# Recurrent heads: the scores of neighbouring pairs as VectorE products summed by ones, and the sums of output squares in a rounded part and its rest

## The chip, the cores and the metric

One core of a Trainium2 chip. The metric is the device time of one execution in microseconds; it was measured in three runs of the kernel before. A profile of one further execution shows where the time goes.

## The reference

A two-layer decoder trunk for 1024 new prompt tokens and 8 sampled tokens. Layer A is a gated linear recurrence (HGRN2) with 8 heads of 128 keys and 128 values, layer B is differential attention; each has a SwiGLU FFN behind it. What matters here is the mixer of layer A, cut to its core:

```
q, f, i, g = jnp.split(xn @ w_in, 4, axis=-1)
fg = lb + (1.0 - lb) * jax.nn.sigmoid(f)
qh, kh, logf, vh = jax.nn.silu(q), 1.0 - fg, jnp.log(fg), i
...
scores = jnp.einsum('bthk,bshk,btshk->bhts', qc, kc, decay)   # decay = exp(b_t - b_s), s <= t
...
o = rmsnorm(o, gnorm.reshape(HG_HEADS, HG_DV))
o = o * jax.nn.silu(g)
return o @ w_out, s_new
```

All of it is float32. A score of token t and an earlier token s is the sum over the 128 keys of q_t, k_s and the product of the forget gates from s + 1 to t.

## The kernel before, in words

Activations lie with features on partitions and the T = 1032 tokens (1024 of the prompt and 8 samples) along the free axis. A projection works on slabs of weights of 128 x 2048 numbers. SyncE loads a slab, GpSimd (POOL) splits it into a rounded part `w_hi` and the rest `w_lo`, and TensorE (PE) makes three rounded (float32r) products per tile with activations split in the same way (`split_product`, lines 728 to 730). A group is one output chunk of 128 features over one of NT = 3 tiles of TS = 344 tokens: 8 x 3 = 24 such products. The other products of the stage are full float32.

The recurrent heads come first in the program. Every head needs 12 projection groups (0 to 2 q, 3 to 5 the gate, 6 to 8 f, 9 to 11 v). PE's order is written out by hand in `hg_head(h)`: the 12 groups of head h + 1 (`next_part`) stand between the small steps of head h, so that PE has work while the other engines prepare the next small step. Every step waits on semaphores that count up. The steps of a head:

- `hg_norm(h - 1)`, line 887: three full-precision products of a matrix of ones with the squares of the last head's output, `RS`. Each gives the sum over 128 features, for 344 tokens. ACT takes Ln and Exp of it (`hg_rstd`, lines 1560 and 1562), DVE multiplies the output by it (`hg_norm`, line 1980), POOL gates it (line 688).
- `hg_diagonal`, line 907: 8 products of K and Q of 128 tokens each; only the diagonals are kept. DVE then multiplies Q by the forget gate F (line 2054) and copies the diagonals into the scores `SA` by a mask (line 2055).
- `hg_turn_v`, line 896: 8 transposes of V into banks 5 and 6, which the sums of `hg_norm` also use, so it waits for the Ln (`hg_oln`). ACT copies them to `VT` (line 1587).
- `hg_level(h, l)` for l = 0 to 6, line 921: the scores between the two halves of blocks of 2, 4, ... 128 tokens, 8 products each. Level 0 is that of neighbouring tokens: it computes 128 x 64 scores per block of 128 tokens, and one per odd token is kept. After each level DVE multiplies decays into Q and K (`hg_spread`, lines 2006 and 2007), makes the next block decays (`hg_totals`, line 1995) and copies the wanted scores (`hg_take`, line 2015).
- `hg_spread_v`, `hg_turn_k`, `hg_sample`, `hg_outer` and `hg_output`: the sample's state, the states of the blocks of 128 and the output, in banks 3 and 4. ACT copies the output to `O` (line 1615) and squares it into `RS` (line 1621).

The last head is `hg_last`: there are no next groups, and the groups of the output projection (`woa_early`, which needs the first six heads' gated outputs reloaded, cast by ACT in line 1571 and split by DVE in line 1942) stand between its steps. Its first, `woa_first`, follows level 0 and takes the six chunks one by one. The table `WOA_AT` says how many groups follow each level. DVE adds their results to the residual (`woa_add`, line 1949). At the end PE has `hg_norm(7)`, six more early groups and `out_late`. `hg_head` of ACT (line 1573 on) and of DVE (line 2049 on) are the same heads as their engines' queues have them; an engine does them in this order and each waits for its own semaphores.

## Time and profile before

| | us |
|---|---|
| median of 3 runs | 2818.02 (2816.6 to 2820.09) |
| the profiled execution | 2818.19 |
| its span, first to last instruction | 2816.5 |
| PE busy | 2750.8 (98%) |
| DVE busy | 1192.1 (42%) |
| ACT busy | 574.3 (20%) |
| POOL busy | 1102.3 (39%) |
| mean granted clock of PE, as a share | 0.990 |

The profile's busy time of an engine is the time in which at least one of its instructions ran. PE's products overlap: one starts while the one before still drains, so what a product costs is the distance from its start to the next one's, not its own duration. A full-precision product is recorded as two instructions (x6 for three products). PEld is PE's weight load and PEq its instruction queue. The bracket behind a row of a timeline gives how long the engine sat idle before it, and what released it.

### The profile page before, as it was taken

Reading aid. Unit: us, or ns where it says so; the run is one execution under the profiler, and the core shown is the slowest. Engines: PE = TensorE matmul, PEld = TensorE weight load, DVE = VectorE, ACT = ScalarE, POOL = GpSimd, SP = SyncE. Lnnn points to the kernel's source line nnn. Section 1 sums busy time; section 2 is a strip of 40 time slices with the busy share of each in tenths; the row PEclk is TensorE's granted clock in tenths of the full one; section 3 lists DMA queues with packets and bytes.
Section 4 is the critical chain, followed back from the end, with each engine's and each line's share of the span. In section 5 each row is a group of like instructions: output and inputs, shape, how many; then the busy total and the mean of one; then the engine's idle time right before and its main releaser. Section 6 shows DMA issues by size and latency. Waiting matters only on the chain.

```text
span 2816.5 us, 43463 instructions
## 1 busy us (share of the span) xinstructions
PE 2750.8 (98%) x17561; PEld 2668.1 (95%) x17561; DVE 1192.1 (42%) x2257; ACT 574.3 (20%) x1182; POOL 1102.3 (39%) x962
## 2 busy tenths in 40 slices
PE   7999999989999999999999999988999999999999
PEld 6999999989999999999999888876899999999999
DVE  4355554455333333333361334476433333333335
ACT  4222222223200000000030233464130000000003
POOL 4333333333444443333346324313533334444334
PEclk8999999999999999999999999999999999999999
DMA  3211111121111111111122111165211111111111
GB/s 106 61 54 54 54 54 54 47 92 54 46 46 45 46 45 47 56 48 45 46 92 68 43 57 52 40 216 189 93 50 45 46 45 46 45 46 45 52 54 61
DMA packets 202241, 175.06 MB, mean 62 GB/s; under 512 B 6290, under 2 KB 185093, under 8 KB 202062
## 3 DMA queue, kind: packets, MB, share of 16 engines
q1 hardware_dynamic: 162592, 141.67, 16.1%
q10 hardware_dynamic: 39470, 30.78, 3.4%
q8 instruction: 140, 2.29, 0.3%
q14 instruction: 39, 0.32, 0.0%
HBM read 147.06 MB, written 25.36 MB: 61 GB/s over the span
## 4 chain that ended last, share of the span: by engine, by line
PE 92%; DVE 4%; ACT 1%; POOL 1%; issue 1%; DMA 0%; ACTq 0%; SPq 0%; PEld 0%; DVEq 0%; PEldq 0%; POOLq 0%
PE ps L728 27%; PE ps L730 26%; PE ps L729 26%; PE ps L921 3%; PE ps L1181 2%; PE ps L1161 2%; DVE act_lo L1942 1%; PE ps L1269 1%; PE ps L907 1%; PE ps L954 1%; PE ps L963 1%; PE ps L887 0%; DVE k_page L2285 0%; PE ps L947 0%; PE ps L1139 0%
## 5 line engine op out<-in xcount | busy, mean ns | idle before, releaser
L728 PE MATMUL ps<-act_hi,w_hi 128*128 128x344 f32 (+2 forms) x3808 | 1243.9, 327 | 26.8 <-DVE act_lo L1914 7.5
L729 PE MATMUL ps<-act_lo,w_hi 128*128 128x344 f32 (+2 forms) x3808 | 1220.7, 321 | 0.0
L730 PE MATMUL ps<-act_hi,w_lo 128*128 128x344 f32 (+2 forms) x3808 | 1220.6, 321 | 0.0
L677 POOL TENSOR_TENSOR w_hi<-w_stage,ones 128x512 fp32r<-128x512 f32 (+1 forms) x412 | 428.4, 1070 | 1285.8 <-PEq L778 1120.4
L728 PEld LDWEIGHTS ps<-act_hi,w_hi 128*128 128x128 f32 x3808 | 718.9, 189 | 44.1 <-issue 32.3
L729 PEld LDWEIGHTS ps<-act_lo,w_hi 128*128 128x128 f32 x3808 | 718.9, 189 | 3.5 <-issue 1.7
L730 PEld LDWEIGHTS ps<-act_hi,w_lo 128*128 128x128 f32 x3808 | 718.8, 189 | 0.0
L681 POOL TENSOR_TENSOR w_lo<-w_stage,w_hi 128x512 fp32r<-128x512 f32 (+1 forms) x412 | 541.5, 1345 | 8.1
L728 PE MATMUL ps<-h_hi,w_hi 128*128 128x344 f32 x1056 | 339.3, 321 | 1.1 <-DVE resid L2123 1.1
L729 PE MATMUL ps<-h_lo,w_hi 128*128 128x344 f32 x1056 | 337.3, 319 | 0.0
L730 PE MATMUL ps<-h_hi,w_lo 128*128 128x344 f32 x1056 | 337.2, 319 | 0.0
L2123 DVE TENSOR_TENSOR resid<-resid,ps 128x344 f32<-128x344 f32 x504 | 258.1, 513 | 180.6 <-PE ps L730 180.2
L2100 DVE TENSOR_TENSOR ps<-ps,rstd 128x344 f32<-128x344 f32 x132 | 68.9, 524 | 391.2 <-PE ps L730 380.5
L1651 ACT ACTIVATE silu_gate<-ps 128x344 f32<-128x344 f32 x132 | 60.1, 458 | 807.2 <-DVE ps L2100 807.2
L2103 DVE TENSOR_TENSOR ps<-ps,rstd 128x344 f32<-128x344 f32 x132 | 69.2, 524 | 363.3 <-PE ps L730 363.3
L728 PEld LDWEIGHTS ps<-h_hi,w_hi 128*128 128x128 f32 x1056 | 198.4, 188 | 2.9 <-DVE resid L2123 2.3
L730 PEld LDWEIGHTS ps<-h_hi,w_lo 128*128 128x128 f32 x1056 | 198.7, 188 | 0.0
L729 PEld LDWEIGHTS ps<-h_lo,w_hi 128*128 128x128 f32 x1056 | 198.5, 188 | 0.0
L1656 ACT CAST h_hi<-ps 128x344 fp32r<-128x344 f32 x132 | 58.9, 446 | 445.3 <-DVE ps L2106 445.3
L921 PEld LDWEIGHTS ps<-hg_q,hg_k 128*128 128x128 f32 (+4 forms) x896 | 93.8, 177 | 4.5 <-issue 3.7
L921 PE MATMUL ps<-hg_q,hg_k 128*128 128x64 f32 (+4 forms) x896 | 94.7, 258 | 2.0 <-DVE hg_scores L2055 1.7
L694 POOL TENSOR_TENSOR state_sample<-state_sample,hg_f 128x1024 f32<-128x1024 f32 x8 | 16.6, 2071 | 193.8 <-DMA state_sample<-in_state_hgrn 193.8
(298 smaller groups left out, 2179.3 us busy)
## 6 DMA issues: line engine op xcount, KB each, us to landing
w_stage<-in_w_gate_up SPq DMA_DIRECT2D x88, 512.0 KB, 5.0
w_stage<-in_w_down SPq DMA_DIRECT2D x44, 512.0 KB, 4.2
w_stage<-in_w_in_a SPq DMA_DIRECT2D x32, 512.0 KB, 5.2
w_stage<-in_w_kv SPq DMA_DIRECT2D x16, 512.0 KB, 4.3
v_page<-in_cache_v SPq DMA_DIRECT2D x16, 512.0 KB, 6.2
w_stage<-in_w_out_b SPq DMA_DIRECT2D x12, 512.0 KB, 4.4
k_page<-in_cache_k SPq DMA_DIRECT2D x10, 512.0 KB, 5.3
x_spill<-resid ACTq DMA_DIRECT2D x8, 516.0 KB, 2.9
```

What stands on the lines that cost most here:

```text
L677: last = g.tensor_tensor(hi[:, part], WST[:, part], ones[:, 0:1].to_broadcast([P, quarter]), ALU.mult)
L681: last = g.tensor_tensor(lo[:, part], WST[:, part], hi[:, part], ALU.subtract)
L728: pe.matmul(out, wh, xh, start=first, stop=False)
L729: pe.matmul(out, wh, xl, start=False, stop=False)
L730: return pe.matmul(out, wl, xh, start=False, stop=last)
L921: last = pe.matmul(PS[0:KEYS[l], 3 + l % 2, c * 64:(c + 1) * 64], K[h % 2][:, c * P:c * P + KEYS[l]], q[:, c, :, 1, :], start=True, stop=True)
L1161: last = pe.matmul(PS[:, bank + k0 // 512, 0:k1 - k0], QA[:, 2 * h + c, n * P:(n + 1) * P], KTB[h % 2][:, c, k0:k1], start=True, stop=True)
L1651: a.activation(SIL[:, tile(t)], PS[:, t, 0:TS], ACT.Silu).then_inc(ffn_silu, 1)
L1656: a.copy(HH[par][:, k, tile(t)], PS[:, 3 + t, 0:TS]).then_inc(ffn_hh, 1)
L2100: v.tensor_tensor(PS[:, t, 0:TS], PS[:, t, 0:TS], RS[:, tile(t)], ALU.mult).then_inc(ffn_gscaled, 1)
L2103: v.tensor_tensor(PS[:, 3 + t, 0:TS], PS[:, 3 + t, 0:TS], RS[:, tile(t)], ALU.mult).then_inc(ffn_uscaled, 1)
L2123: v.tensor_tensor(X[:, m, tile(t)], X[:, m, tile(t)], PS[:, 6 + q % 2, 0:TS], ALU.add).then_inc(ffn_down_free, 1)
```

## The change

It does three things, for each head.

1. Level 0 is no longer made from K and Q by PE. DVE multiplies the forget gate of the odd tokens, K of the even and Q of the odd ones into `PR` (two products of 128 x 512), ahead of the diagonal. PE sums them over the keys with one full-precision product with the ones (128 x 512), which gives each score in every row; the same mask picks it. `hg_spread(h, 0)` no longer waits for PE's level 0, and `hg_take` gets that wait.
2. The squares of the output are rounded by ACT into `OHI` (in the memory of `HKT`, k_tok), and DVE takes the rest, in place, into `RSL`. PE sums both with rounded ones: 6 rounded products for 3 full ones.
3. The order: on PE group 0 of the next head comes before `hg_norm(h - 1)`, and group 1 before `hg_turn_v`; ACT takes group 0 before `hg_rstd` and group 1 before the copies of V. In `hg_last` nothing of this order changes.

```
--- before.py
+++ after.py
@@ -109,6 +109,7 @@
         WL = [place(f"w_lo{s}", [P, SLAB], F32R) for s in range(2)]
         rs_at = cursor[0]
         RS = place("rstd", [P, T])
+        RSL = at("square_lo", [P, T], F32R, rs_at)
         ident = place("ident", [P, P])
         ones = place("ones", [P, P])
         pick = place("pick", [P, 16])
@@ -178,6 +179,7 @@
         hg_k_ready = sem("hg_k_ready")
         hg_diag_full = sem("hg_diag_full")
         hg_qp_ready = sem("hg_qp_ready")
+        hg_pairs_ready = sem("hg_pairs_ready")
         hg_tot = sem("hg_tot")
         hg_p_full = sem("hg_p_full")
         hg_spread_done = sem("hg_spread_done")
@@ -199,6 +201,7 @@
         hg_os_full = sem("hg_os_full")
         hg_os_copied = sem("hg_os_copied")
         hg_osq = sem("hg_osq")
+        hg_osq_lo = sem("hg_osq_lo")
         hg_on_full = sem("hg_on_full")
         hg_oln = sem("hg_oln")
         hg_ors = sem("hg_ors")
@@ -337,12 +340,16 @@
         assert w[0] >= arena + (NB + 1) * D * 4
         VT = part("v_tok", [P, NB, P])
         SA = part("hg_scores", [P, SEQ])
-        HKT = part("k_tok", [P, NB, P])
+        hkt_at = w[0]
+        OHI = part("o_square_hi", [P, T], F32R)
+        HKT = at("k_tok", [P, NB, P], F32, hkt_at)
         ST = part("hg_states", [P, NB, P])
         S0 = part("state_sample", [P, DEC, P])
         TOT = [None] + [part(f"block_decay{l}", [P, SEQ >> l]) for l in range(1, NL + 1)]
         lmask = [part(f"level_mask{l}", [P, P // 2], BF16) for l in range(NL)]
         dmask = part("diagonal_mask", [P, P], BF16)
+        PR = part("pair_products", [P, SEQ // 2])
+        onesr = part("ones_rounded", [P, P], F32R)
 
         SQN = 6
         SQ = at("squares", [P, SQN, T], F32, arena + 65536 - SQN * T * 4)
@@ -649,6 +656,7 @@
             step(g.affine_select(out=dmask[:], in_=dmask[:], compare_op=ALU.not_equal, fill=1.0,
                                  base=0, pattern=[[-1, P]], channel_multiplier=1))
             step(g.memset(SA[:], 0.0))
+            step(g.tensor_tensor(onesr[:], ones[:], ones[:], ALU.mult))
             g.memset(stat[:], 0.0).then_inc(consts, 1)
 
             def split(n, cols=SLAB, gain=None):
@@ -881,10 +889,13 @@
 
             def hg_norm(h):
 
-                pe.wait_ge(hg_osq, h + 1)
+                pe.wait_ge(hg_osq, 2 * h + 2)
                 pe.wait_ge(hg_state_ready, (h + 1) * NB)
                 for t in range(NT):
-                    last = pe.matmul(PS[:, 5 + t, 0:TS], ones[:], RS[:, tile(t)], start=True, stop=True)
+                    pe.matmul(PS[:, 5 + t, 0:TS], onesr[:], OHI[:, tile(t)], start=True, stop=False)
+                pe.wait_ge(hg_osq_lo, h + 1)
+                for t in range(NT):
+                    last = pe.matmul(PS[:, 5 + t, 0:TS], onesr[:], RSL[:, tile(t)], start=False, stop=True)
                 last.then_inc(hg_on_full, 1)
 
             def hg_turn_v(h):
@@ -911,11 +922,13 @@
             def hg_level(h, l):
 
                 half = LEVELS[l] // 2
-                if l:
-                    pe.wait_ge(hg_spread_done, h * NL + l)
-                else:
-                    pe.wait_ge(hg_qp_ready, h + 1)
-                pe.wait_ge(hg_s_ready, h * (NL + 1) + max(l, 1))
+                if l == 0:
+                    pe.wait_ge(hg_pairs_ready, 2 * h + 2)
+                    pe.wait_ge(hg_s_ready, h * (NL + 1) + 1)
+                    pe.matmul(PS[:, 3, :], ones[:], PR[:], start=True, stop=True).then_inc(hg_p_full, 1)
+                    return
+                pe.wait_ge(hg_spread_done, h * NL + l)
+                pe.wait_ge(hg_s_ready, h * (NL + 1) + l)
                 q = Q[h % 2][:, 0:SEQ].rearrange("p (c n u m) -> p c n u m", c=NB, u=2, m=half)
                 for c in range(NB):
                     last = pe.matmul(PS[0:KEYS[l], 3 + l % 2, c * 64:(c + 1) * 64], K[h % 2][:, c * P:c * P + KEYS[l]],
@@ -1056,12 +1069,12 @@
 
                 def next_part(q):
                     hg_part(h + 1, q)
+                next_part(0)
                 if h:
                     hg_norm(h - 1)
-                next_part(0)
                 hg_diagonal(h)
+                next_part(1)
                 hg_turn_v(h)
-                next_part(1)
                 for l in range(NL):
                     hg_level(h, l)
                     if l == 1:
@@ -1572,8 +1585,6 @@
 
             def hg_head(h, more):
 
-                if more and h:
-                    hg_rstd(h - 1)
                 act.wait_ge(hg_os_full, h)
                 act.wait_ge(s1_out, h * 16)
                 act.dma_start(S0[:], state_in[h]).then_inc(s0_in, 16)
@@ -1581,12 +1592,15 @@
                     hg_rstd(h - 1)
                 if more:
                     hg_evacuate(h + 1, 0)
+                    if h:
+                        hg_rstd(h - 1)
+                    hg_evacuate(h + 1, 1)
                 act.wait_ge(hg_o_full, h * 2)
                 for u in range(2):
                     act.wait_ge(hg_vt_full, h * 2 + u + 1)
                     a.copy(VT[:, 4 * u:4 * u + 4, :], PS[:, 5 + u, :].rearrange("p (b n) -> p b n", b=4)).then_inc(hg_vt_ready, 1)
                 if more:
-                    for q in range(1, 9):
+                    for q in range(2, 9):
                         hg_evacuate(h + 1, q)
                     hg_gates(h + 1)
                 if not more:
@@ -1598,6 +1612,7 @@
                 act.wait_ge(hg_s1_ready, (h + 1) * DEC)
                 act.dma_start(state_out[h], S0[:]).then_inc(s1_out, 16)
                 act.wait_ge(hg_kv_full, h)
+                act.wait_ge(hg_on_full, h)
                 for u in range(2):
                     act.wait_ge(hg_kst_full, h * 2 + u + 1)
                     a.copy(HKT[:, 4 * u:4 * u + 4, :], PS[:, 5 + u, :].rearrange("p (b n) -> p b n", b=4)).then_inc(hg_kst_ready, 1)
@@ -1619,6 +1634,9 @@
                 act.wait_ge(hg_os_copied, h + 1)
                 act.wait_ge(hg_on, h)
                 a.activation(RS[:], O[:], ACT.Square).then_inc(hg_osq, 1)
+                act.wait_ge(hg_osq, 2 * h + 1)
+                act.wait_ge(hg_kv_full, h + 1)
+                a.copy(OHI[:], RS[:]).then_inc(hg_osq, 1)
                 if more:
                     hg_evacuate(h + 1, 11)
 
@@ -1974,6 +1992,11 @@
                     sum_square(norm_ph, m)
 
 
+            def hg_square_rest(h):
+
+                dve.wait_ge(hg_osq, 2 * h + 2)
+                v.tensor_tensor(RSL[:], RS[:], OHI[:], ALU.subtract).then_inc(hg_osq_lo, 1)
+
             def hg_norm(h):
 
                 dve.wait_ge(hg_ors, h + 1)
@@ -2000,7 +2023,10 @@
                 fine = TOT[l] if l else F
                 tot = fine[:, 0:2 * n].rearrange("p (n u) -> p n u", u=2)
                 q, k = hg_pairs(Q[h % 2][:, 0:SEQ], l)[:, :, 1, :], hg_pairs(K[h % 2][:, 0:SEQ], l)[:, :, 0, :]
-                dve.wait_ge(hg_p_full, h * NL + l + 1)
+                if l:
+                    dve.wait_ge(hg_p_full, h * NL + l + 1)
+                else:
+                    dve.wait_ge(hg_pairs_ready, 2 * h + 2)
                 dve.wait_ge(hg_qp_ready, h + 1)
                 dve.wait_ge(hg_spread_done, h * NL + l)
                 v.tensor_tensor(q, q, tot[:, :, 0:1].to_broadcast([P, n, half]), ALU.mult)
@@ -2011,6 +2037,7 @@
                 keys = KEYS[l]
                 s = hg_pairs(SA[0:keys, :], l)[:, :, 1, :].rearrange("p (c n) m -> p c n m", c=NB)
                 m = lmask[l][0:keys, :].bitcast(U16).rearrange("p (n m) -> p n m", m=LEVELS[l] // 2).unsqueeze(1)
+                dve.wait_ge(hg_p_full, h * NL + l + 1)
                 dve.wait_ge(hg_s_ready, h * (NL + 1) + l + 1)
                 v.copy_predicated(s, m.to_broadcast([keys, NB, P // LEVELS[l], LEVELS[l] // 2]),
                                   PS[0:keys, 3 + l % 2, :].rearrange("p (c n m) -> p c n m", c=NB, m=LEVELS[l] // 2)
@@ -2050,6 +2077,13 @@
 
                 dve.wait_ge(hg_k_ready, h + 1)
                 hg_totals(h, 0)
+                if h:
+                    hg_square_rest(h - 1)
+                odd, even = (hg_pairs(x[:, 0:SEQ], 0)[:, :, u, 0] for x, u in ((F, 1), (K[h % 2], 0)))
+                v.tensor_tensor(PR[:], odd, even, ALU.mult).then_inc(hg_pairs_ready, 1)
+                dve.wait_ge(hg_pairs_ready, 2 * h + 1)
+                v.tensor_tensor(PR[:], PR[:], hg_pairs(Q[h % 2][:, 0:SEQ], 0)[:, :, 1, 0], ALU.mult).then_inc(hg_pairs_ready, 1)
+                dve.wait_ge(hg_pairs_ready, 2 * h + 2)
                 dve.wait_ge(hg_diag_full, h + 1)
                 v.tensor_tensor(Q[h % 2][:, 0:SEQ], Q[h % 2][:, 0:SEQ], F[:, 0:SEQ], ALU.mult).then_inc(hg_qp_ready, 1)
                 v.copy_predicated(SA[:].rearrange("p (c n) -> p c n", c=NB),
@@ -2080,6 +2114,7 @@
             hg_head(HEADS - 1, last=True)
             woa_add(12, 6)
             woa_rest(EARLY, XL32[:, EARLY, :])
+            hg_square_rest(HEADS - 1)
             hg_norm(HEADS - 1)
             dve.wait_ge(hg_on, HEADS)
             v.tensor_tensor(O[:], O[:], G[(HEADS - 1) % 2][:], ALU.mult).then_inc(hg_head_done, 1)
```

What stands in DVE's queue where head 1 begins (behind the states of head 0 and before the diagonal scores are used), before; `hg_f` is the forget gate, `block_decay` the products of neighbouring gates:

```order
L1995 TENSOR_TENSOR block_decay_96<-hg_f 128x512 [waits hg_tot,hg_k_ready]
L2054 TENSOR_TENSOR hg_q_83<-hg_q_83,hg_f 128x1024 [waits hg_diag_full]
L2055 COPY_PREDICATED hg_scores<-diagonal_mask,ps 128x1024
L2006 TENSOR_TENSOR hg_q_83<-hg_q_83,hg_f 128x512 [waits hg_spread_done,hg_qp_ready,hg_p_full]
L2007 TENSOR_TENSOR hg_k_85<-hg_k_85,hg_f 128x512
L1995 TENSOR_TENSOR block_decay_97<-block_decay_96 128x256 [waits hg_tot]
L2015 COPY_PREDICATED hg_scores<-level_mask_103,ps 128x512 [waits hg_s_ready]
```

And after the change:

```order
L2018 TENSOR_TENSOR block_decay_98<-hg_f 128x512 [waits hg_tot,hg_k_ready]
L1998 TENSOR_TENSOR square_lo<-rstd,o_square_hi 128x1032 [waits hg_osq]
L2083 TENSOR_TENSOR pair_products<-hg_f,hg_k_86 128x512
L2085 TENSOR_TENSOR pair_products<-pair_products,hg_q_84 128x512 [waits hg_pairs_ready]
L2088 TENSOR_TENSOR hg_q_84<-hg_q_84,hg_f 128x1024 [waits hg_diag_full,hg_pairs_ready]
L2089 COPY_PREDICATED hg_scores<-diagonal_mask,ps 128x1024
L2032 TENSOR_TENSOR hg_q_84<-hg_q_84,hg_f 128x512 [waits hg_spread_done,hg_qp_ready,hg_pairs_ready]
L2033 TENSOR_TENSOR hg_k_86<-hg_k_86,hg_f 128x512
L2018 TENSOR_TENSOR block_decay_99<-block_decay_98 128x256 [waits hg_tot]
L2042 COPY_PREDICATED hg_scores<-level_mask_105,ps 128x512 [waits hg_s_ready,hg_p_full]
```

Three instructions came in ahead of the wait for the diagonal (`hg_diag_full`), and the wait for PE's level 0 (`hg_p_full`) moved from the spread to the copy of the scores.

DVE's queue at the end of the last head, behind its states, before (`resid` are the adds of the output projection, `act_lo` the rests of its operands):

```order
L1949 TENSOR_TENSOR resid<-resid,ps 128x344 [waits woa_full] x6
L1942 TENSOR_TENSOR act_lo<-act_whole,act_hi 128x1032 [waits hi_ready]
L1980 SCALAR_TENSOR_TENSOR hg_o<-hg_o,vectors,rstd 128x1032 [waits hg_ors]
L2085 TENSOR_TENSOR hg_o<-hg_o,hg_gate_87 128x1032 [waits hg_on]
L1949 TENSOR_TENSOR resid<-resid,ps 128x344 [waits woa_full] x4
```

And after the change:

```order
L1967 TENSOR_TENSOR resid<-resid,ps 128x344 [waits woa_full] x6
L1960 TENSOR_TENSOR act_lo<-act_whole,act_hi 128x1032 [waits hi_ready]
L1998 TENSOR_TENSOR square_lo<-rstd,o_square_hi 128x1032 [waits hg_osq]
L2003 SCALAR_TENSOR_TENSOR hg_o<-hg_o,vectors,rstd 128x1032 [waits hg_ors]
L2120 TENSOR_TENSOR hg_o<-hg_o,hg_gate_88 128x1032 [waits hg_on]
L1967 TENSOR_TENSOR resid<-resid,ps 128x344 [waits woa_full] x4
```

The rest of the squares stands behind the sixth add, whose group is the last that PE makes before the norm, and behind the rest of chunk 6. On PE the norm of the last head, between the 18th and 19th group of the output projection, reads after the change:

```order
L738 MATMUL ps<-act_hi,w_lo_57 128x344
L895 MATMUL ps<-o_square_hi,ones_rounded 128x344 [waits hg_state_ready,hg_osq]
L895 MATMUL ps<-o_square_hi,ones_rounded 128x344 x2
L898 MATMUL ps<-square_lo,ones_rounded 128x344 [waits hg_osq_lo]
L898 MATMUL ps<-square_lo,ones_rounded 128x344 x2
L736 MATMUL ps<-act_hi,w_hi_56 128x344 [waits woa_free,operand_split,w_split]
```

Where three full-precision products stood that waited for the squares alone, there are now three and three, and the second three wait for DVE.

## Rows read from the trace of the kernel before

**Rows 1.** The page, chain of work that ended last, by engine.
```profile
PE 92%; DVE 4%; ACT 1%; POOL 1%; issue 1%; DMA 0%; ACTq 0%; SPq 0%; PEld 0%; DVEq 0%; PEldq 0%; POOLq 0%
```

**Rows 2.** Busy time by stretch, one head: from:to, us, busy us, PE's clock, DMA.
```profile
292.00:361.60 69.60, 69.60 (x509) 68.71 (x509) 35.30 (x47) 19.55 (x28) 25.18 (x18) 1.00 0.20 55
```

**Rows 3.** PE's waits from 60 to 700 us: total, times, longest.
```profile
PE ps L728 <- DVE act_lo L1942: 5.5, 2, 5.2
PE ps L728 <- DVE resid L1949: 2.7, 2, 1.9
PE ps L921 <- DVE hg_scores L2055: 1.7, 1, 1.7
```

**Rows 4.** Timeline of PE at a norm: start, us, instruction.
```profile
291.82 1.90 PE L887 MATMUL ps<-rstd,ones 128*128 128x344 f32 x6
...
293.71 0.32 PE L729 MATMUL ps<-act_lo,w_hi 128*128 128x344 f32 x1
...
294.34 0.32 PE L730 MATMUL ps<-act_hi,w_lo 128*128 128x344 f32 x1
```

**Rows 5.** Timeline of PE at level 0 of the same head.
```profile
303.76 1.89 PE L921 MATMUL ps<-hg_q,hg_k 128*128 128x64 f32 x16
...
305.71 0.32 PE L729 MATMUL ps<-act_lo,w_hi 128*128 128x344 f32 x1
```

**Rows 6.** Timeline of PE, two 512-column sums with the ones in the FFN.
```profile
719.36 1.02 PE L744 MATMUL ps<-rstd,ones 128*128 128x512 f32 x2
...
721.24 0.32 PE L729 MATMUL ps<-act_lo,w_hi 128*128 128x344 f32 x1
```

**Rows 7.** Timeline of ACT in one head: table load, Ln, square.
```profile
292.50 1.28 ACT L1560 ACT_TABLE_LOAD   x1
293.79 1.12 ACT L1560 ACTIVATE rstd<-ps,eps_col 128x1032 f32<-128x1032 f32 x1
...
358.49 1.06 ACT L1621 ACTIVATE rstd<-hg_o 128x1032 f32<-128x1032 f32 x1
```

**Rows 8.** Timeline of DVE in one head, from the diagonal on.
```profile
299.31 2.90 DVE L2054 TENSOR_TENSOR hg_q<-hg_q,hg_f 128x1024 f32<-128x1024 f32 x1 [14.14 <-PE ps L907]
302.12 1.32 DVE L2055 COPY_PREDICATED hg_scores<-diagonal_mask,ps 128x1024 f32<-128x1024 uint16 x1
...
354.11 0.68 DVE L1995 TENSOR_TENSOR block_decay<-hg_f 128x512 f32<-128x512 f32 x1
```

**Rows 9.** Timeline of POOL, the first split of weights.
```profile
19.76 1.04 POOL L677 TENSOR_TENSOR w_hi<-w_stage,ones 128x512 fp32r<-128x512 f32 x1 [8.23 <-DMA w_stage<-in_w_in_a]
```

**Rows 10.** The chain of waits, front of the last head: start, us, what.
```profile
576.47 1.98 PE ps L921 x16
...
578.47 0.69 DVE hg_q L2006
...
582.37 1.04 DVE act_lo L1942
...
583.43 11.60 DVE act_lo L1942 x5
```

**Rows 11.** Timeline of ACT, the Exp in the front of the last head.
```profile
574.60 1.06 ACT L1562 ACTIVATE rstd<-rstd 128x1032 f32<-128x1032 f32 x1
```

**Rows 12.** Timeline of PE, DVE and POOL at the last norm.
```profile
660.05 1.90 PE L887 MATMUL ps<-rstd,ones 128*128 128x344 f32 x6
...
660.68 1.23 DVE L1942 TENSOR_TENSOR act_lo<-act_whole,act_hi 128x1032 fp32r<-128x1032 f32 x1
...
662.00 4.04 POOL L677 TENSOR_TENSOR w_hi<-w_stage,ones 128x512 fp32r<-128x512 f32 x4 [14.94 <-PEq L778]
```

**Rows 13.** Timeline of PE, behind a wait early in the stage.
```profile
49.24 0.40 PE L728 MATMUL ps<-act_hi,w_hi 128*128 128x344 f32 x1 [2.19 <-ACT hg_q L1543]
```

**Rows 14.** Busy time by stretch, columns as in rows 2.
```profile
50.00:54.00 4.00, 4.00 (x18) 4.00 (x17) 0.00 (x0) 0.00 (x0) 4.00 (x4) 0.57 0.00 0
600.00:602.00 2.00, 0.79 (x5) 0.82 (x6) 2.00 (x5) 0.00 (x0) 0.10 (x1) 1.00 0.28 49
```

More of the change, by code:

```diff
@@ L882, in hg_norm @@
             def hg_norm(h):
-                pe.wait_ge(hg_osq, h + 1)
+                pe.wait_ge(hg_osq, 2 * h + 2)
                 pe.wait_ge(hg_state_ready, (h + 1) * NB)
                 for t in range(NT):
-                    last = pe.matmul(PS[:, 5 + t, 0:TS], ones[:], RS[:, tile(t)], start=True, stop=True)
+                    pe.matmul(PS[:, 5 + t, 0:TS], onesr[:], OHI[:, tile(t)], start=True, stop=False)
+                pe.wait_ge(hg_osq_lo, h + 1)
+                for t in range(NT):
+                    last = pe.matmul(PS[:, 5 + t, 0:TS], onesr[:], RSL[:, tile(t)], start=False, stop=True)
                 last.then_inc(hg_on_full, 1)
@@ L1573, in hg_head @@
             def hg_head(h, more):
-                if more and h:
-                    hg_rstd(h - 1)
                 act.wait_ge(hg_os_full, h)
@@ L1588, in hg_head @@
                 if more:
-                    for q in range(1, 9):
+                    for q in range(2, 9):
                         hg_evacuate(h + 1, q)
@@ L1621, in hg_head @@
                 a.activation(RS[:], O[:], ACT.Square).then_inc(hg_osq, 1)
+                act.wait_ge(hg_osq, 2 * h + 1)
+                act.wait_ge(hg_kv_full, h + 1)
+                a.copy(OHI[:], RS[:]).then_inc(hg_osq, 1)
                 if more:
```

47 lines of the change are left out of this document (38 added, 9 removed).

## The prediction

> **What bounds the kernel now.** I read first, on the page, the chain of work that ended last, then the busy table of one head, then the list of waits, then the timelines of single engines at the places that the diff touches. PE holds 92% of it [rows 1]; the rest is small and spread. In the stage of the recurrent heads this is complete: in the 69.6 us of one head PE is busy for 69.60, at a granted clock of 1.00, while DVE has 35.30, ACT 19.55 and POOL 25.18 [rows 2]. Between 60 and 700 us PE waits for three things only, 9.9 us in all, and all of them in the last head [rows 3]. So in heads 0 to 6 a microsecond taken from PE is a microsecond of the kernel as long as nothing new is late, and the last head has to be walked through.
>
> **Norm sums.** In a head the three full-precision sums of the squares begin at 291.82; the GEMM behind them has its second product at 293.71, one spacing after its first, and spacings of the GEMM are 0.157 (four from 293.71 to 294.34). The sums therefore take 293.71 - 0.157 - 291.82 = 1.73 us [rows 4]. After the change six rounded products of the same 344 columns do it. They have the shape and type of the GEMM's own, so 6 x 0.157 = 0.94 us. Gain 0.79 us per norm.
>
> **Level 0.** The eight score products of level 0 take from 303.76 to 305.71 - 0.16 = 305.55, 1.79 us [rows 5]. One full-precision product with the ones over 512 columns replaces them. The nearest rows are the two 512-column sums with the same ones in the first FFN: 719.36 to 721.24 - 0.16 = 721.08 for two, 0.86 each [rows 6]. Gain 0.93 us per head.
>
> **What the other engines get, and what covers it.** ACT rounds the squares, one more pass over 1032 elements; the square itself has 1.06 us [rows 7], and I take the same. It also loads one table more per head (1.28 [rows 7]), since a silu now stands ahead of the Ln. DVE makes the rest of the squares (1.23, by the equal subtraction at 660.68 [rows 12]) and two products over 512 alternating elements (0.68 each, by the equal block decay product [rows 8]), 2.6 us per head. POOL makes the rounded ones once, and 512 columns cost it 1.04; it idles for 8.23 us right behind, until the first weights land [rows 9]. I take nothing; without that cover it would be 0.3 us. The covers, counted from T, the end of the last projection group (291.82 here, 361.4 one head later):
> - The square ends at 358.49 + 1.06 = 359.55, T - 1.9 [rows 7]; rounding ends at T - 0.8 and the rest at T + 0.5. PE now does a projection group of 24 x 0.157 = 3.76 first and wants the rest at T + 4.2. Slack 3.7 us; without that group it would be a stall, and in the last head there is no such group.
> - ACT evacuates group 0 at T + 3.9 to T + 5.7 (table load and, as an estimate from the square's 1.06 us for three times as many elements, 0.5), then loads the table and takes the Ln (1.28 and 1.12 [rows 7]), done at T + 8.1. The transposes of V, which overwrite what the Ln reads, start after group 1 at T + 3.76 + 0.94 + 1.79 + 3.76 = T + 10.3. Slack 2.2 us.
> - DVE multiplies Q by F and copies the diagonal scores as before; at worst 2.90 and 1.32 us [rows 8], which ended 0.3 us before level 0 began at 303.76. Group 1 and the transposes stand between diagonal and level 0 in either order, so this slack stays 0.3. The products are ready by T + 2, before the diagonal; DVE was idle for 14.1 us there [rows 8].
> So heads 0 to 6 get all: 7 x 0.93 = 6.5 for level 0 and, as head 0 has no norm ahead of it, 6 x 0.79 = 4.7 for the norms.
>
> **The front of the last head** has no group 0, and is a chain, not PE's work. T is 570.2. By the same steps the rest is ready at T + 0.6, PE's second three sums end at T + 1.1 (not T + 1.7), the diagonal at T + 2.9. DVE's product and copy then take 2.5, so level 0 starts at T + 5.7, where it was T + 6.3 (576.47) [rows 10]. Level 0 takes 0.86 instead of 1.79, and DVE's spread (two products of 0.69 and a block decay of 256 elements, 1.6 us from 578.47 on [rows 10]), which used to wait for it, runs meanwhile. So DVE takes level 0's scores about 2.8 us earlier, and with that come earlier the norm, the first rest (582.37) and the chain of six rests that PE then follows one by one (11.60 us for five [rows 10], slowed by POOL, whose work is released by the same norm and so moves along). Gain 2.8 us. ACT's Exp, which the norm needs, ended at 574.60 + 1.06 = 575.7 [rows 11] and comes no later now; the norm asks for it at 578.3.
>
> **The last norm** is where a new wait appears. PE reached it at 660.05 [rows 12] and went on 1.73 later, at 661.78. In DVE's order the new subtraction stands behind the add of the last finished output group and the rest of chunk 6 (660.68, 1.23) [rows 12]; it runs from 661.85 to 663.1. PE does its three rounded sums, idles for 2.6 us and ends the other three at 663.15 + 0.47 = 663.6: loss 1.8 us instead of a gain of 0.8. POOL's split, which began at 662.00 [rows 12], is released by PE beyond this norm and so starts after the subtraction. Everything behind (Ln, Exp, norm, gate, the last six output groups) keeps its distance from PE's end of the sums; PE waits behind it only for those adds, 0.8 of the 2.7 us [rows 3], so the loss stays.
>
> **The clock there.** PE's granted clock is 1.00 nearly throughout, but after a wait of 2.19 us at 49.24 it fell from 2.4 to 1.2 GHz for a while [rows 13]: 0.57 as the mean of the 4 us from 50 to 54 [rows 14]. That is 4 x 0.43 = 1.7 us of full clock lost, and at most that of time. After the longest wait for DVE's adds, 1.9 us [rows 3], it stayed at 1.00 [rows 14]. The new wait of 2.6 us is nearer to the first: I take a loss of 1.5, with 0 and 1.7 as its ends. The Trainium skill ("TensorE: Matmul & The Clock Gate", "HAM oscillation") tells to fear only idle gaps longer than this one; by it the 1.5 would be nothing. The trace's 2.19 us speaks against that, and the row decides.
>
> **Sum.** 6.5 + 4.7 + 2.8 - 1.8 - 1.5 = 10.7 us. The profiled execution took 2818.19, so 2807.5 (the median of the runs, 2818.02, lies 0.17 below it, which I neglect). A measurement tells about 0.2%, 5.6 us, from no change.
>
> **Rivals.**
> - *The clock holds at the last norm*: 2806.0. For it, one wait of 1.9 us without a fall; against it, the fall after 2.19. Chance 0.20.
> - *The tail costs more.* If POOL's split does overlap the new subtraction, this takes what the rests beside POOL took, 2.3 on average (11.60 / 5 [rows 10]), instead of 1.23: 1.1 us more, up to 2 for a worse one: 2808.6 to 2809.5. The Trainium skill ("SBUF — State Buffer", "Who interferes with whom") states that such a subtraction with both inputs in SBUF and a GpSimd operation lock each other out; the rests beside POOL agree. For it: the two are 0.1 us apart. Against it: PE's order releases POOL later. Chance 0.12.
> - *The last head's front gives back little* (the rests wait for the casts or for loads from memory that don't move earlier): the 2.8 becomes 0 to 1, 2809.5 to 2810.5. Against it: the casts stand in ACT's queue right behind the Exp of rows 11, and a cast is shorter than a rest beside POOL. Chance 0.08.
> - *The heads come to wait for DVE*: the level 0 copy has only 0.3 us. With 0.5 to 1 us per head for seven heads the gain falls by 3.5 to 7: 2811 to 2814.5. Against it: the same operations stand between in both orders. Chance 0.07.
> - *Slower: ACT's longer queue holds the transposes of V.* Their Ln now stands behind the silu of group 0 and its table. It has 2.2 us of slack; from a delay of 2.2 + 1.72 = 3.9 us on, a head loses more than it gained. At 6 us late it would be 3.8 - 1.72 = 2.1 lost in each of six heads; with 0.9 and 2.8 gained in head 0 and the front and 3.3 lost at the tail, about 2830. ACT is idle for 50 of 69.6 us [rows 2], so nothing names such a delay. Chance 0.03.
> - *The change doesn't do what it says*: sums through rounded ones run at the price of full-precision sums, 6 x 0.577 = 3.47 instead of 1.73, as the three before took 0.577 each. Then six norms lose 1.74 instead of gaining 0.79, the front gains about nothing, and the last norm ends 3.0 late (663.1 + 1.73): 2818.2 + 10.4 - 6.5 + 3.0 = 2825. Chance 0.02; the type is that of the GEMM.
>
> The forecast keeps 0.48. The range 2804.0 to 2811.0 takes in the first three rivals and the bounds of the clock's cost, and 1.5 us on either side for what runs differ (2816.6 to 2820.09 before). Under 2812.4 the kernel is faster by over 0.2%: everything but most of the DVE rival's upper half and the last two, 0.92. Slower 0.05, the same 0.03.
>
> **What would show it.** In the profile after: head periods of 67.9 us with PE busy throughout; six rounded sums in 0.94 us, a 512-column product of 0.86 us between transposes of V and group 2; no wait for ACT or DVE in heads 0 to 6; in the last head the first of the rests 2.8 us earlier from the start of its norm; one new PE wait of about 2.6 us for the squares' rest, and half clock behind it. The prediction is wrong if a wait stands before the transposes of V or before level 0 in every head, or if the time behind the last norm catches up.

## The result, and the profile after

| us | before | after |
|---|---|---|
| median of 5 runs, side by side | 2818.16 (2816.6 to 2820.58) | 2804.93 (2800.62 to 2805.55) |
| the profiled execution | 2818.19 | 2805.55 |
| its span | 2816.5 | 2803.8 |
| PE / ACT / DVE busy | 2750.8 / 574.3 / 1192.1 | 2736.3 / 591.2 / 1196.7 |

The ratio is 0.9947, with an interval from 0.9936 to 0.9959. The kernel is faster: 12.6 us by the two profiled executions, 13.2 by the medians, where 10.7 was forecast. The direction held and the size did not: 2818.02 x 0.9947 is 2803.1, 0.9 us under the low end of the range, 2804.0. The miss is small beside the interval, which reaches from 2800.0 to 2806.5 by the same product, and the median itself, 2804.93, lies inside the range. What has to be explained is the 2 to 3 us by which the gain was forecast too small. Six executions in the runs below took over 3000 us, two of them of the kernel before, and are left out of every median, mean and ratio.

A steady head is the busy table from one norm to the next, beside [rows 2]. The three stretches below it are the clock's (span of the stretch, then busy us of each engine, and the granted clock):

```profile
core 0: us, PE busy (x) PEld busy (x) DVE busy (x) ACT busy (x) POOL busy (x), PEclk, DMA share, GB/s
289.92:357.80 67.88, 67.88 (x496) 67.09 (x495) 35.49 (x50) 21.80 (x30) 25.21 (x18) 1.00 0.20 56
50.00:54.00 4.00, 4.00 (x27) 4.00 (x26) 0.00 (x0) 0.46 (x1) 4.00 (x4) 1.00 0.00 0
649.00:653.00 4.00, 4.00 (x18) 4.00 (x17) 0.70 (x1) 3.24 (x3) 3.92 (x5) 0.57 0.00 0
584.00:588.00 4.00, 3.27 (x12) 3.30 (x13) 3.34 (x6) 0.00 (x0) 1.99 (x2) 0.57 0.15 43
```

67.9 us per head instead of 69.6, PE busy throughout. PE's timeline shows where it comes from, beside [rows 4, 5]:

```profile
289.92 0.64 PE L895 MATMUL ps<-o_square_hi,ones_rounded 128*128 128x344 f32 x3
290.39 0.63 PE L898 MATMUL ps<-square_lo,ones_rounded 128*128 128x344 f32 x3
290.87 1.95 PE L918 MATMUL ps<-hg_q,hg_k 128*128 128x128 f32 x16
...
296.42 1.04 PE L907 MATMUL ps<-ident,hg_v 128*128 128x128 f32 x8
297.29 1.02 PE L928 MATMUL ps<-pair_products,ones 128*128 128x512 f32 x2
297.75 0.72 PE L736 MATMUL ps<-act_hi,w_hi 128*128 128x344 f32 x1
298.31 0.32 PE L737 MATMUL ps<-act_lo,w_hi 128*128 128x344 f32 x1
```

The six rounded sums take 290.87 - 289.92 = 0.95. The GEMM's second product comes at 298.31, one spacing after its first, so the pair sums take 298.31 - 0.157 - 297.29 = 0.86. The covers on DVE and ACT, in the same head:

```profile
285.37 1.23 DVE L1998 TENSOR_TENSOR square_lo<-rstd,o_square_hi 128x1032 fp32r<-128x1032 f32 x1 [5.88 <-ACT o_square_hi L1639]
286.52 0.68 DVE L2083 TENSOR_TENSOR pair_products<-hg_f,hg_k 128x512 f32<-128x512 f32 x1
287.24 0.69 DVE L2085 TENSOR_TENSOR pair_products<-pair_products,hg_q 128x512 f32<-128x512 f32 x1
```

```profile
292.92 1.23 DVE L2088 TENSOR_TENSOR hg_q<-hg_q,hg_f 128x1024 f32<-128x1024 f32 x1 [4.99 <-PE ps L918]
294.06 1.32 DVE L2089 COPY_PREDICATED hg_scores<-diagonal_mask,ps 128x1024 f32<-128x1024 uint16 x1
```

```profile
293.25 1.13 ACT L1573 ACTIVATE rstd<-ps,eps_col 128x1032 f32<-128x1032 f32 x1
```

The rest of the squares is there at 286.6, 3.8 us before PE takes it at 290.39. The Ln is done at 294.4 and the transposes of V start at 296.42: 2.0 us of slack. DVE's copy of the diagonal scores ended at 295.38, 1.9 us before level 0 at 297.29. So nothing waits in heads 0 to 6, and PE's list of waits between 60 and 700 us holds the last head alone, as in [rows 3]:

```profile
PE ps L736 <- DVE act_lo L1960: 3.8, 1, 3.8
PE ps L736 <- DVE resid L1967: 3.3, 2, 2.5
PE ps L898 <- DVE square_lo L1998: 2.4, 1, 2.4
PE ps L928 <- DVE hg_scores L2089: 1.4, 1, 1.4
PE ps L907 <- ACT rstd L1573: 0.2, 1, 0.2
```

The third line is the new wait, at the last norm. On PE, DVE and POOL there, beside [rows 12]:

```profile
644.94 0.63 PE L895 MATMUL ps<-o_square_hi,ones_rounded 128*128 128x344 f32 x3
648.00 0.74 PE L898 MATMUL ps<-square_lo,ones_rounded 128*128 128x344 f32 x3 [2.42 <-DVE square_lo L1998]
648.57 0.32 PE L736 MATMUL ps<-act_hi,w_hi 128*128 128x344 f32 x1
...
649.51 0.49 PE L738 MATMUL ps<-act_hi,w_lo 128*128 128x344 f32 x1
```

```profile
645.57 1.23 DVE L1960 TENSOR_TENSOR act_lo<-act_whole,act_hi 128x1032 fp32r<-128x1032 f32 x1
646.71 1.23 DVE L1998 TENSOR_TENSOR square_lo<-rstd,o_square_hi 128x1032 fp32r<-128x1032 f32 x1
```

```profile
648.79 4.04 POOL L685 TENSOR_TENSOR w_hi<-w_stage,ones 128x512 fp32r<-128x512 f32 x4 [16.82 <-PEq L786]
```

PE idles for 2.42 us for the subtraction that stands second in DVE's queue, and then falls to 1.2 GHz: 0.57 from 649 to 653. POOL starts 0.85 us after the subtraction is done, so the two don't meet.

**The ledger.** The same points of the program in the two profiles, and what each stretch gave:

| point | before | after | change in the stretch |
|---|---|---|---|
| restart behind the first 2.19 us wait [rows 13] | 49.24 | 49.41 | +0.2 |
| end of the last projection group, head 1 | 152.67 | 150.41 | -2.4 |
| the same, last head (T) | 570.17 | 557.63 | -10.3 |
| last norm reached | 660.05 | 644.94 | -2.6 |
| PE past the last norm | 661.78 | 648.57 | +1.9 |
| `out_late` reached | 679.75 | 668.08 | +1.5 |
| end of the span | 2816.5 | 2803.8 | -1.0 |

(For head 1, after's norm begins at 154.17, with one more group of 3.76 ahead of it. "Past the last norm" is the start of the second product behind it less one spacing of 0.157, as above.) The third line is six heads of 1.71. The second should be one level 0, 0.93. The other 1.5 is a fall of the clock that before had at 50 us [rows 14] and after, behind the same wait, had not: 1.00 above. And a further 1.0 came where no instruction differs. These two amounts, 2.5 us, are what the forecast lacked of this pair of profiles: with them taken out, 12.7 - 2.5 leaves 10.2.

### The profile page after: what moved, and what is told of

Its sections match the earlier page's. It is cut to its first block, busy times and chain, and to the rows that moved or that the text cites. A ratio compares the mean times of both kernels' runs of the same rounds, so it can differ in the third digit from the quotient of the medians.

```text
span 2803.8 us, 43350 instructions
## 1 busy us (share of the span) xinstructions
PE 2736.3 (98%) x17449; PEld 2656.2 (95%) x17449; DVE 1196.7 (43%) x2281; ACT 591.2 (21%) x1196; POOL 1100.9 (39%) x963
## 4 chain that ended last, share of the span: by engine, by line
PE 93%; DVE 4%; POOL 1%; ACT 1%; issue 1%; DMA 1%; SPq 0%; PEld 0%; DVEq 0%; ACTq 0%; PEldq 0%; POOLq 0%
PE ps L736 27%; PE ps L738 27%; PE ps L737 27%; PE ps L934 3%; PE ps L1194 2%; PE ps L1174 2%; PE ps L1282 1%; PE ps L918 1%; PE ps L967 1%; PE ps L976 1%; PE ps L1152 0%; PE ps L960 0%; DVE k_page L2320 0%; PE ps L979 0%; DMA x_stage<-in_x_prompt 0%
## 5 line engine op out<-in xcount | busy, mean ns | idle before, releaser
L677 POOL TENSOR_TENSOR w_stage<-w_stage,vectors 128x512 f32<-128x512 f32 x48 | 50.5, 1083 | 89.3 <-DMA w_stage<-in_w_kv 43.6
L2032 DVE TENSOR_TENSOR hg_q<-hg_q,block_decay 128x512 f32<-128x512 f32 x48 | 44.4, 925 | 95.2 <-PE ps L934 95.2
```

## The experiments

All ran with five timed runs or more each, beside runs of the kernel before on the same chip. They fall into three batches on three chips: the first four experiments, the next four (from old_order on), and the last four (after_third, tail_second, both_second, all_three). Medians are compared within a batch unless the text says otherwise.

### The two kernels again

> The kernel before, once more. If the clock falls behind a wait by chance from execution to execution, its profile shows the half clock at other waits than the first profile (there at 50 to 54 us, 579 to 590, and four places in the second layer), and its times scatter by 2 to 4 us; ratio 0.9990 to 1.0010. If the falls belong to the kernel, the same places again and a scatter under 1 us.

2818.19 us, ratio 0.9997 (0.9987 to 1.0006). The clock fell in another place:

```profile
50.00:54.00 4.00, 4.00 (x28) 4.00 (x27) 0.00 (x0) 0.46 (x1) 3.79 (x4) 1.00 0.02 4
600.00:604.00 4.00, 4.00 (x18) 4.00 (x17) 1.29 (x2) 0.00 (x0) 0.00 (x0) 0.57 0.49 166
```

Both rows are the other way round in [rows 14]: the same kernel, the same waits, other falls, and the same total. What a fall costs can be read from it. This profile restarts behind the first wait at 48.67 instead of 49.24 and reaches T at 568.09 instead of 570.17: 2.08 - 0.57 = 1.5 us for the fall at 50. At the last norm (659.55 for 660.05) 1.6 of that is gone again, for the one at 600.

> The changed kernel, once more. Its first profile had no half clock behind the wait of 2.2 us at 49.4 where the kernel before had one (worth 1.4), and one behind each of three waits in the last head. Chance: the places change, ratio to before 0.9940 to 0.9960. A steady gain of the last head's front (the six rests not held up by POOL): the six rests take under 8 us again, as against 12.7 before.

2805.26 us, ratio 0.9949 (0.9935 to 0.9962). The wait of 2.42 us and the fall behind it came again; the six rests took 12.74 us as in before, so their short time in the first profile was not steady. Against the second profile of before, each of six heads gives 1.72, the last norm costs 1.9 and the fall about 1.5. The front shows 4.4 from T to the last norm, 1.6 of it the fall that before's second profile had there, so 2.8.

### The two parts by themselves

```
# level0_alone: before, with the pair products and hg_level(h, 0) of the change
+        PR = part("pair_products", [P, SEQ // 2])
...
+                if l == 0:
...
+                    pe.matmul(PS[:, 3, :], ones[:], PR[:], start=True, stop=True).then_inc(hg_p_full, 1)
+                    return
...
# squares_alone: after, with these undone; the split squares and the new order stay
```

> Level 0 through DVE's products alone, in the order of before. By the terms of the prediction 8 x 0.93 less what the front of the last head hides, plus about 1.9 there for the spread that no longer waits: 8 to 9 us, 2809.5, ratio 0.9970. If the pair products hold up the diagonal's follow-up in DVE's queue, less than 6. Head period 69.56 - 0.93 = 68.6.

2808.88 us, ratio 0.9963 (0.9950 to 0.9977): 10.0 us gained by the medians, where 8 to 9 were expected. A head takes 68.69, with PE busy throughout:

```profile
287.01:355.70 68.69, 68.69 (x496) 67.30 (x495) 36.12 (x49) 19.56 (x28) 25.21 (x18) 1.00 0.20 56
```

> The two-part sums of squares with the new order, level 0 as before. 6 x 0.79 = 4.7, about 0.6 in the front, 1.9 lost at the last norm and 1.5 behind it by the clock: 1.9 to 3.4 us faster, ratio 0.9990. Head period 69.56 - 0.79 = 68.8. If the two parts don't add up, level0_alone and this one together give less than 9 or more than 14 us, where the change gave 13.

2814.51 us, ratio 0.9985 (0.9976 to 0.9994): 4.4 gained, where 1.9 to 3.4 were expected; its ten runs scatter by 3 us. Its head, from norm to norm:

```profile
292.56:361.37 68.81, 68.81 (x510) 68.50 (x509) 34.84 (x48) 21.78 (x30) 25.18 (x18) 1.00 0.19 55
```

So per head 0.9 and 0.8, as the sum had them. Six norms give about 4.7 us, and the last norm takes back 1.9 of it: the profile of squares_alone shows that wait (2.4 us), in this execution without a fall behind it. The front is level 0's: from T to the last norm squares_alone takes 90.3 us and before 89.9, level0_alone 89.2 with a fall of 1.5 in it that before's first profile had not, so 87.7. 10.0 + 4.4 = 14.4 us, where the whole change gave 13.6 in the same batch. That is a little over the 14 us above which squares_alone's expectation would have said that the parts don't add up. But the difference of 0.8 is within the scatter, and by the places each part gives its own share, so no interplay between them is shown or needed.

### The order of the steps

```
# old_order: after, with PE's and ACT's order of before
-                next_part(0)
                 if h:
                     hg_norm(h - 1)
+                next_part(0)
                 hg_diagonal(h)
-                next_part(1)
                 hg_turn_v(h)
+                next_part(1)
... (ACT's order likewise)
```

> The changed kernel with the order of before in heads 0 to 6 (norm ahead of group 0, V turned ahead of group 1; ACT's rstd ahead of group 0). If the slack of 3.7 us that group 0 gives was needed, PE waits 0.5 us or more in each of six heads for the squares' rest, 3 us or more lost against the change. By the steps of the last head, where there is no group 0 either, the rest ends at T + 0.55 and PE asks for it at T + 0.5: under 0.2 us per head, 0 to 1 us lost, ratio 0.9953.

2806.60 us, ratio 0.9963 (0.9950 to 0.9975), on a chip where before had 2817.63: 11.0 us gained, where the change gave 13.2, 13.6 and 11.9 in its three comparisons. PE's timeline at the norm:

```profile
286.02 0.64 PE L895 MATMUL ps<-o_square_hi,ones_rounded 128*128 128x344 f32 x3
286.54 0.74 PE L898 MATMUL ps<-square_lo,ones_rounded 128*128 128x344 f32 x3
290.89 1.95 PE L918 MATMUL ps<-hg_q,hg_k 128*128 128x128 f32 x16
```

The second sums start 0.52 after the first instead of 0.47. That is the whole wait for the rest, which is ready almost in time even without a projection group ahead. A head takes 68.03 us here, as the mean of five, and 67.88 after the change: 0.15 more, so a further 0.1 lies elsewhere in the order. Followed through its profile, the old order is at most 1.0 us behind by the last head, and 0.4 at the end. The 2 us by the medians are within the uncertainty. The prediction took the group for the cover without which there "would be a stall"; by its own T + 0.5 against T + 0.47, it was one of less than 0.1 us.

### The last norm's wait

```
# tail_early, tail_second: after, with DVE's last steps in another order
-            woa_add(12, 6)
+            woa_add(12, 3)
+            hg_square_rest(HEADS - 1)
+            woa_add(15, 3)
             woa_rest(EARLY, XL32[:, EARLY, :])
-            hg_square_rest(HEADS - 1)
```

> The changed kernel, with the rest of the last head's squares three adds earlier in DVE's queue (behind the add of group 14, ahead of those of 15 to 17 and of chunk 6's rest). If the wait of 2.4 us at the last norm and the half clock behind it are what the text says, both go: 2.5 + 1.4 = 3.9 us against the change, about 2801.3, ratio 0.9936. If the time is caught up behind it anyway (the adds, the loads), nothing moves. If the clock falls without that wait, 2.5.

2803.84 us, ratio 0.9955 (0.9943 to 0.9968). PE at the last norm, and the clock in three stretches:

```profile
646.37 0.63 PE L895 MATMUL ps<-o_square_hi,ones_rounded 128*128 128x344 f32 x3
646.84 0.63 PE L898 MATMUL ps<-square_lo,ones_rounded 128*128 128x344 f32 x3
647.31 0.32 PE L736 MATMUL ps<-act_hi,w_hi 128*128 128x344 f32 x1
```

```profile
50.00:54.00 4.00, 4.00 (x18) 4.00 (x17) 0.00 (x0) 0.00 (x0) 4.00 (x4) 0.57 0.00 0
585.00:589.00 4.00, 2.97 (x10) 3.00 (x11) 3.65 (x6) 0.00 (x0) 2.28 (x2) 0.61 0.12 28
648.00:652.00 4.00, 4.00 (x27) 4.00 (x26) 1.18 (x2) 2.99 (x3) 4.00 (x4) 1.00 0.00 0
```

The sums take 0.94 with no wait, and the clock stays at 2.4 GHz: from the last norm to `out_late` 19.2 us instead of 23.1. That shows that the wait is DVE's order, and the fall did not come without the wait. But this profile has falls at 50 and at 585, and the ratio lies among those of the changed kernel (0.9947 to 0.9956), so no gain of the whole is shown here, where 3.9 was expected. The repeat, beside a third run of the changed kernel:

> The changed kernel a third time, to compare the next three with on one chip and to see how often the clock falls at which wait. Ratio 0.9940 to 0.9956. If the falls are by chance, the total of half-clock time in its profile differs again from the first two (54 and 47 us) by some multiple of 3.4 us.

2806.73 us, ratio 0.9956 (0.9943 to 0.9968). The half clock in its profile is 57.4 us in all, after 54.1 and 47.2 in the first two: it differs again.

> The squares' rest earlier, again. In the first profile PE gained 3.6 us at the place itself, but the median moved only 1 us, since the profile had more falls of the clock elsewhere. If that was chance, this median lies 2.5 to 3.9 us under the changed kernel's. If the gain is given back by something steady, it lies within 1.5 again, and the profile shows where.

2802.86 us, ratio 0.9948 (0.9935 to 0.9961): 3.9 us under after_third, as was expected if chance had hidden the gain, and 19.2 us from the last norm to `out_late` again. Over all runs, though, the changed kernel has a mean of 2804.9 (15 runs) and this one 2803.9 (10 runs), each with a standard deviation over 2. The local gain is shown; how much of it reaches the whole is not settled.

### The last head's front

```
# front_rests_first: after; on DVE in the last head at level 0 the order is
#   hg_take, the six woa_rest, hg_norm(h - 1)
# instead of hg_take, hg_norm(h - 1), the six woa_rest
```

The page of the Trainium skill "SBUF — State Buffer" ("Who interferes with whom") says that such a DVE subtraction and a POOL operation that reads SBUF exclude each other, and that the order of issue decides who is held up. The two profiles of the changed kernel show what that does to the six rests. Here DVE and POOL of the first:

```profile
566.91 6.95 DVE L1960 TENSOR_TENSOR act_lo<-act_whole,act_hi 128x1032 fp32r<-128x1032 f32 x6
```

```profile
567.08 9.06 POOL L696 TENSOR_TENSOR hg_o<-hg_o,hg_gate 128x1032 f32<-128x1032 f32 x1 [33.16 <-DVE hg_o L2003]
```

and of the second:

```profile
566.40 12.74 DVE L1960 TENSOR_TENSOR act_lo<-act_whole,act_hi 128x1032 fp32r<-128x1032 f32 x6
```

```profile
566.56 3.32 POOL L696 TENSOR_TENSOR hg_o<-hg_o,hg_gate 128x1032 f32<-128x1032 f32 x1 [33.15 <-DVE hg_o L2003]
```

The same instructions, started at the same distance, and once DVE goes through at its own pace while POOL's gate takes 9.06 us, once the gate takes 3.32 and the six rests 12.74, beside the gate and the POOL operations behind it. By both profiles the exclusion that the Trainium skill states agrees. But DVE's first rest starts 0.16 to 0.17 us ahead of the gate both times, so the order in which the two began does not tell who is held up over the six. The norm releases the gate, so rests put ahead of it can't meet it.

> The changed kernel, with DVE's six rests in the front of the last head ahead of the norm of head 6, so that POOL's gate, which the norm releases, does not run beside them. If POOL is what stretches them to 12.7 us, they take 7 us as once by chance, and PE reaches level 1 2 to 3 us earlier: 2802.8, ratio 0.9942. If PE's half clock (2.6 us a chunk) is the pace there, only the 1.2 us of the norm. If POOL's splits become late through it, PE waits for slab 17 and the gain is lost.

2799.39 us, ratio 0.9939 (0.9926 to 0.9951). DVE and POOL:

```profile
565.28 6.97 DVE L1960 TENSOR_TENSOR act_lo<-act_whole,act_hi 128x1032 fp32r<-128x1032 f32 x6
572.18 1.28 DVE L2003 SCALAR_TENSOR_TENSOR hg_o<-hg_o,vectors,rstd 128x1032 f32<-128x1032 f32 x1
```

```profile
573.54 2.42 POOL L696 TENSOR_TENSOR hg_o<-hg_o,hg_gate 128x1032 f32<-128x1032 f32 x1 [40.07 <-DVE hg_o L2003]
```

PE waits 2.7 us for the first rest instead of 3.8, and the gate has its 2.42 us alone. From T to the last norm it takes 83.4 us instead of 87.3, and the clock held behind the last norm's wait in this profile, 1.5 more. The median, 5 to 7 us under the changed kernel's in the other batches, has about that; 2802.8 had been expected.

> Both of the moves. They touch different places: 3.9 + 2.3 = 6 us against the change, about 2799, ratio 0.9928, if each does what is expected of it alone.

2798.95 us, ratio 0.9936 (0.9923 to 0.9949), as expected. Repeated, in the last batch:

> Both moves again. By the places: 3.6 + 5 = 8 to 9 us under the changed kernel if chance is all that hid the tail's part, 5 to 6 if the tail gives nothing to the whole time.

2799.97 us, ratio 0.9934 (0.9921 to 0.9947), 6.8 under after_third, between the two outcomes named. Over all runs this pair has a mean of 2799.2 (10 runs), 5.7 under the changed kernel. front_rests_first alone has 2799.9 (5 runs): of the 3.9 us at the last norm, 0.7 shows here.

All fourteen profiles side by side show what the front's time hangs on (us; the six rests, the first groups of the output projection from their start to level 1, the wait for adds at level 1, and whether the clock fell behind that):

| profile | rests | first groups | wait | fell | T to last norm |
|---|---|---|---|---|---|
| before | 12.73 | 12.9 | 1.85 | no | 89.9 |
| before_again | 12.75 | 13.0 | 1.87 | yes | 91.5 |
| squares_alone | 12.75 | 13.0 | 1.85 | no | 90.3 |
| level0_alone | 12.75 | 12.9 | 1.85 | yes | 89.2 |
| after | 6.95 | 11.2 | 2.50 | yes | 87.3 |
| after_again | 12.74 | 13.0 | 1.84 | no | 87.1 |
| after_third | 6.94 | 11.2 | 2.46 | yes | 87.4 |
| tail_early | 6.95 | 11.3 | 2.36 | yes | 87.4 |
| old_order | 6.94 | 10.9 | 1.82 | yes | 86.5 |
| tail_second | 6.95 | 9.9 | 1.75 | no | 84.0 |
| front_rests_first | 6.97 | 10.1 | 2.17 | no | 83.4 |
| tail_and_front | 6.98 | 11.3 | 1.71 | no | 84.2 |
| both_second | 6.97 | 10.1 | 2.18 | no | 83.4 |
| all_three | 6.97 | 9.9 | none | no | 80.9 |

The six rows from after to tail_second have one and the same front in code. Where the rests take 6.9 they are not the pace of the first groups. PE is busy without a break there, and what differs is how long it stays at 1.2 GHz behind its wait of 3.8 us for the first rest. The busy table of after and of tail_second over these groups:

```profile
568.29:579.46 11.17, 11.17 (x54) 11.17 (x55) 5.57 (x5) 2.06 (x2) 11.17 (x4) 0.74 0.15 60
569.48:579.38 9.90, 9.90 (x55) 9.90 (x56) 5.57 (x5) 1.96 (x2) 9.90 (x3) 0.85 0.16 64
```

The front takes 84.0 when the rests are short, the half clock of the first groups is too and no fall comes at level 1, and 2.5 to 3.4 us more when that is not so. Rests ahead of the norm make the short rests certain. The clock stays a chance at both places: at level 1 it held three times of three, and in tail_and_front the first groups took 11.3 again.

What stood next were PE's two waits for DVE's adds at level 1: PE doesn't start its next output groups until DVE has read their banks, and DVE does the long `hg_spread` first.

```
# all_three: both edits, and in the last head for l > 0
+            woa_add(*WOA_AT[l - 1])
             hg_spread(h, l)
-            woa_add(*WOA_AT[l - 1])
```

> Both moves, and in the last head DVE's adds of the finished output groups ahead of each level's spread, since it is idle while PE works on the level. PE waited 2.2 us (1.7 in the other profile) for such an add at level 1. That wait goes: 1.7 to 2.2 us, with a fall of the clock behind it 3.5; against both moves alone 1.5 to 3.5 us, ratio 0.992 to 0.993. If the adds hold up the spread that level 2 needs, nothing or a loss.

2796.03 us, ratio 0.9922 (0.9910 to 0.9935), 10.7 under after_third and 3.9 under both_second (1.5 to 3.5 expected), the best of all; 80.9 us from T to the last norm. PE's waits between 60 and 700 us:

```profile
PE ps L736 <- DVE act_lo L1960: 2.7, 1, 2.7
PE ps L928 <- DVE hg_scores L2089: 1.4, 1, 1.4
PE ps L736 <- DVE resid L1967: 0.8, 1, 0.8
PE ps L934 <- DVE hg_k L2033: 0.5, 1, 0.5
PE ps L907 <- ACT rstd L1573: 0.2, 1, 0.2
```

The wait for adds at level 1 is gone; one of 0.5 for the spread took its place. 5.6 us of waits are left, of 11.1 after the change and 9.9 before it. The half clock over the whole profile is 40.5 us here, against 54.1 in the changed kernel's first profile and 58.0 in before's.

## Why the prediction was right, and where wrong

The mechanisms came as forecast. The step that failed is the sum, with its range: it took every fall of the clock but the new one from one profiled execution as fixed.

- **Norm sums and level 0**: right. 0.95 and 0.86 were measured for 0.94 and 0.86, a head gives 1.71 for 1.72, and each part by itself gives its own share.
- **Covers**: right. Slack was 3.8 us for the squares' rest (3.7 forecast) and 2.0 for the Ln (2.2). ACT's rounding took 1.06. For DVE's copy of the diagonal the prediction kept 0.3 us; it was 1.9 in the head shown, since the multiplication ahead of it took 1.23 and not 2.90. No wait came in heads 0 to 6, so the rivals of DVE and of ACT's queue did not occur, and neither did the full price for rounded sums. That the rest would stall PE without the moved group was wrong in effect: old_order shows a wait under 0.1 us a head, and 0.15 for the whole order.
- **Front of the last head**: 2.6 (after) and 2.8 (after_again) for 2.8. after_again took the stated road: rests of 12.74 us as before, everything 2.8 earlier. In after's profile the agreement is luck: the rests took 6.95, so that level 1 began at T + 21.8 instead of T + 26.4 (after_again: T + 23.6), and then a wait of 2.5 us for adds with half clock behind it (584 to 588 above) gave that back. Where the clock also rises sooner in the first groups and holds at level 1, as in tail_second, the same front gains 89.9 - 84.0 = 5.9. "POOL moves along" held for its start and not for the rests' pace, and the term, put as one number, hides a spread of 3 us between executions. The rival in which the front gives back little did not occur.
- **Last norm**: right in mechanism and size. 1.9 for 1.8, the wait 2.42 for 2.6, half clock behind it, 1.5 for 1.5. tail_early takes the wait away and both costs vanish. The rival of POOL's overlap fell: its split began after the subtraction. The rival in which the clock holds did not come in the three profiles of the change nor in old_order. But in squares_alone and front_rests_first, with the same 2.4 us wait, the clock held. So this too is a chance, only a high one.
- **Sum**: this is the step that failed. It was made against one profiled execution and took all its falls of the clock but the new one as fixed. Before's profile had one of 1.5 us behind the 2.19 us wait; it came in 5 of 14 profiles of this study, after_third's among them, and not in after's first. Another 1.0 came behind `out_late`, where the instructions are the same. In the pair of profiles these 2.5 us are the whole difference between the 10.7 forecast and the 12.6 measured, less 0.5 by which the terms came out smaller. The range had "1.5 us on either side for what runs differ"; two such falls together are twice that. Over many executions a fall that either kernel can have cancels, so the 13.5 us by the means are not explained by it: see below.
- **A slip in a rival**: with the front's 2.8 down to 0 to 1, the prediction's own sum gives 2809.3 to 2810.3, not 2809.5 to 2810.5. Nothing hangs on it.

**What stays open.** The stretch from 1307.8 us of before's profile to its end, where no instruction differs, took 1504.8 and 1504.7 us up to the last product in the two profiles of before and 1502.3 to 1504.2 in twelve of the other kernels. Up to the end of the span it took 1508.6 and 1509.2 against 1506.7 to 1508.7, so the two groups touch. It may be that the earlier part of the kernel shifts how often the clock falls there, and nothing tried here tells that from chance. By means over all runs before has 2818.4 (59 runs) and after 2804.9 (15 runs), 13.5 us. The two profiles of before and the three of after differ by 12.4 us on average, 1.2 of it behind `out_late`. The terms as forecast, with the sizes measured, give 0.9 + 10.3 + 2.7 - 1.9 - 1.5 = 10.5 of it; the front's better executions, the executions in which the clock holds at the last norm, and falls elsewhere have to make up the other 3, in shares that the runs don't settle.

## What to carry to other kernels

Where PE is busy without a break, price its edits by start-to-start spacings and believe the sum: it held to hundredths. At the end of such a stretch, where there is no work left to cover, look at the order inside the helper engine's queue instead: a short subtraction behind two unrelated steps cost more (3.4 us) than the change won there, and three reorderings in DVE's queue without any new arithmetic gave another 8.7 us (the mean of all_three, 2796.2, against 2804.9). And when PE has waits of about 2 us, a sum made from one profile can be off by one clock fall (1.5 us here) for each of them, in both directions; read a second profile before you fix the range.

## What the runs showed of the hardware

- **Behind the same wait the clock falls in some executions and holds in others.** After the wait of 2.2 us near 49 us, PE fell from 2.4 to 1.2 GHz in 5 of 14 profiles; after waits of 1.7 to 2.5 us for the adds of level 1, in 6 of 13; after 2.4 us at the last norm, in 4 of 6. Each such fall cost about 1.5 us. The length of the wait alone doesn't decide it: at level 1 it fell behind 1.82 and held behind 2.18. What does decide it, no run here shows. By the Trainium skill ("TensorE: Matmul & The Clock Gate", "HAM oscillation") only longer gaps should matter; these rows stand against it, and the measurement decides.
- **Who wins between DVE and POOL varies.** With POOL's gate released by the norm just ahead of them, the same six subtractions took 12.7 us in five profiles, with the gate at 3.3, and 6.9 in five others, with the gate at 9.1. Alone they took 7.0 and the gate 2.4, in the four profiles that have them ahead of the norm. So a duration read beside a POOL operation was one of two prices.
